# A decoder layer's first feed-forward unit: x and its first weights loaded in quarters over two queues, token squares taken by ScalarE from x as loaded, x in six other PSUM banks

## The chip, the cores and the metric

The kernel runs on one core of one Trainium2 chip. The metric is the device time of one execution in microseconds, and the time before is the median of three runs. The engines are TensorE (PE, matrix products; PEld is its loading of the stationary operand), VectorE (DVE), ScalarE (ACT), GpSimd (POOL) and SyncE (SP, which here only issues transfers).

## What is computed

One layer on x of 512 tokens by 1024 features, all in float32: x plus half a SwiGLU feed-forward, plus a mixer (NSA attention and dilated attention, gated), plus half a second SwiGLU feed-forward, and a final RMSNorm. The change touches only the beginning:

```python
def rmsnorm(x, g):
    y = x32 * lax.rsqrt(jnp.mean(x32 * x32, axis=-1, keepdims=True) + NORM_EPS) * g
...
x = x + 0.5 * swiglu(rmsnorm(x, norm_ffn1[l]), ffn1_w_in[l], ffn1_w_out[l])
```

where `swiglu(h, w_in, w_out)` is `(silu(u) * v) @ w_out` with `u, v` the halves of `h @ w_in` (2 x 2816 columns).

## The kernel before

**Numbers.** Every float32 operand of a large product is split in two rounded parts, `hi` and `lo`, and a product is three passes, hi·hi, lo·hi and hi·lo (`three_pass`, lines 1245 to 1252). ScalarE makes `hi` (an activation Copy into a rounded type), VectorE makes `lo` (original minus `hi`). x is kept transposed, features on partitions, in `xT` (8 feature tiles m of 128 x 512 tokens), times the norm's gain in `xg_hi` and `xg_lo`. The reciprocal root of the mean square is a row over the tokens, so it is not in the operand: it multiplies the products when they are read from PSUM (`rstd_row`, `evac` of `dve_ffn`, line 945).

**Units.** The up projection runs in 22 units of 128 gate and 128 value columns, each 2 x 8 blocks of 128x128 weights, 2 x 512 KB, in two slots of `w_raw`, `w_hi` and `w_lo`. A unit is 48 products of 128x512. SyncE issues the loads of unit f when the low part of unit f-2 is done (`lo_ready`, line 525); ScalarE splits when TensorE has left the slot (`act_split`), VectorE after it (`dve_split`). Unit f from 2 on also waits until the gate of unit f-2 has been scaled (line 1332). The down projection, the mixer and the second feed-forward follow in the same way, each paced by semaphores of the work before.

**The opening** is written out by hand.

- Loads: GpSimd issues the four gains and cmp_pos (five small transfers, lines 621 to 623), all counted on `vec_landed`. SyncE issues x in eight transfers, first the features 0 to 511 for four token blocks, then 512 to 1023 (`x_halves`, line 547), then unit 1. ScalarE issues the constants (with the identity) and unit 0's weights in two halves by feature (`act_load_first`, line 663), then loads its table.
- TensorE (lines 1531 to 1541): five warm-up products on zeros, float32 and so two records each; the transpose of gains and cmp_pos to bank 7, which waits for all five small transfers; 32 transposes of x, tile m to PSUM bank m (`pe_first_transposes`, line 1299), 16 for each half of x; then unit 0.
- Unit 0 goes feature tile by feature tile (`two_products`, line 1290): for each k three passes of gate and three of value into banks 0 and 1. It waits for the half of the low weights and for `g_lo`. As banks 0 and 1 hold x's first two tiles, it also waits until these are copied to `xT` (`x_new`, line 1317).
- Unit 1 accumulates in banks 2 and 3, so it waits for four copies, and for the squares of those tiles. Between its gate and value products stand the column sums (`pe_col`, eight tiny products of `sumsq` with ones) and, after half of the value, the row (`pe_row`, eight products with a diagonal of the reciprocal roots).
- ScalarE (lines 815 to 833): high part of weights half 0; then for each m the high part of x from PSUM (`act_first_hi`), the second weights half after m = 3, and the squares of each feature tile (`act_square`) among them, the high part of unit 1 after m = 6.
- VectorE (lines 1153 to 1173): copy of the gains from bank 7, low part of weights half 0; for each m the low part of x, copies 0 and 1 behind the first two, low half 1 after m = 3; low part of unit 1; copies 2 to 7; then `dve_rstd`.
- GpSimd adds the eight squared feature tiles over m into `sumsq` (`pool_squares`, line 577); the column product then sums over the partitions.

## Time and profile before

| | us |
|---|---|
| median of 3 runs | 1212.22 (1211.77 to 1212.42) |
| the profiled execution | 1211.73 |
| its span in the trace | 1209.9 |
| TensorE busy | 1191.8 (99%) |
| VectorE, ScalarE, GpSimd busy | 570.8, 411.2, 183.2 |

Times in the trace are microseconds from the start of the span. Busy time counts an instruction from its start to its end, and products overlap, so the distance of two starts says more of the pace than their duration. "Idle before <-" names the work that ended an engine's idle time. A timeline merges equal instructions that follow each other (x4). The clock column of the profile shows 1.00 throughout the opening, so the level of TensorE's clock there is read from the distance of its instructions.

### The profile page before, as it was taken

The page shows a single profiled execution, that of the slowest core. Times are in us where ns is not written, and L with a number is a line of the kernel's source. Part 1 is how long each engine was busy: PE and PEld are TensorE (multiplying, and loading weights), DVE is VectorE, ACT ScalarE, POOL GpSimd, SP SyncE. Part 2 cuts the span into 40 slices and gives each one's busy share as a digit, 9 for nine tenths or more (in the row PEclk, how much of TensorE's full clock was granted, in tenths as well). Part 3 has the DMA queues.
Part 4 walks back from the last instruction along what each step waited for, and adds up shares of the span by engine and source line. Part 5 has one row for each costly group of instructions (what it writes and reads, how often), then busy time and mean ns, then how long its engine had stood idle before and what let it go on. Part 6 is the DMA issues. An engine that isn't in the chain of part 4 may idle for free.

```text
span 1209.9 us, 15613 instructions
## 1 busy us (share of the span) xinstructions
PE 1191.8 (99%) x6077; PEld 971.1 (80%) x6077; DVE 570.8 (47%) x898; ACT 411.2 (34%) x578; POOL 183.2 (15%) x205
## 2 busy tenths in 40 slices
PE   8999999999999999999999999999999999999997
PEld 6888888888888988777776788888888888888886
DVE  5544444453333656566656644454544444442222
ACT  5332222322223134443545542233323233222222
POOL 5000000000002571356552000011000000000000
PEclk9999999999999999999999999999999999999998
DMA  7332333223336621222121133333323332223321
GB/s 223 105 94 81 103 104 104 73 81 96 95 107 176 161 77 45 60 60 60 43 75 30 37 95 96 96 105 105 88 86 104 104 102 77 87 76 98 100 84 69
DMA packets 211246, 110.80 MB, mean 92 GB/s; under 512 B 32064, under 2 KB 207600, under 8 KB 211200
## 3 DMA queue, kind: packets, MB, share of 16 engines
q1 hardware_dynamic: 204656, 103.92, 29.9%
q0 software_dynamic: 4288, 5.06, 1.5%
q10 hardware_dynamic: 2256, 1.18, 0.3%
q8 instruction: 32, 0.52, 0.2%
q14 instruction: 14, 0.11, 0.0%
HBM read 105.12 MB, written 2.10 MB: 89 GB/s over the span
## 4 chain that ended last, share of the span: by engine, by line
PE 92%; DVE 4%; ACT 2%; issue 1%; DMA 0%; POOL 0%; DVEq 0%; ACTq 0%; POOLq 0%
PE ps L1250 22%; PE ps L1252 21%; PE ps L1251 21%; PE ps L1358 7%; PE ps L1359 7%; PE ps L1357 7%; PE ps L1460 2%; PE ps L1483 1%; PE ps L1428 1%; PE ps L1441 1%; DVE ps L1056 1%; ACT w_hi L657 1%; DVE w_lo L901 1%; ACT probs L759 1%; PE ps L1495 1%
## 5 line engine op out<-in xcount | busy, mean ns | idle before, releaser
L901 DVE TENSOR_TENSOR w_lo<-w_raw,w_hi 128x2048 fp32r<-128x2048 f32 (+4 forms) x116 | 227.6, 1962 | 410.0 <-ACT w_hi L657 409.7
L1250 PE MATMUL ps<-xg_hi,w_hi 128*128 128x512 f32 x992 | 390.8, 394 | 0.9 <-issue 0.8
L1252 PE MATMUL ps<-xg_hi,w_lo 128*128 128x512 f32 x992 | 386.5, 390 | 0.0
L1251 PE MATMUL ps<-xg_lo,w_hi 128*128 128x512 f32 x992 | 386.3, 389 | 0.0
L657 ACT ACTIVATE w_hi<-w_raw 128x2048 fp32r<-128x2048 f32 (+2 forms) x105 | 182.4, 1737 | 333.4 <-PE ps L1252 210.6
L1250 PEld LDWEIGHTS ps<-xg_hi,w_hi 128*128 128x128 f32 x992 | 186.1, 188 | 48.3 <-issue 10.7
L1252 PEld LDWEIGHTS ps<-xg_hi,w_lo 128*128 128x128 f32 x992 | 186.2, 188 | 39.1
L1251 PEld LDWEIGHTS ps<-xg_lo,w_hi 128*128 128x128 f32 x992 | 186.3, 188 | 37.7
L1357 PE MATMUL ps<-p_hi,w_hi 128*128 128x512 f32 x352 | 137.0, 389 | 0.0
L1359 PE MATMUL ps<-p_hi,w_lo 128*128 128x512 f32 x352 | 137.0, 389 | 0.0
L1358 PE MATMUL ps<-p_lo,w_hi 128*128 128x512 f32 x352 | 136.9, 389 | 0.0
L584 POOL COPY sumsq<-square 128x512 f32<-128x512 f32 x4 | 2.7, 680 | 669.0 <-ACT square L696 666.9
L1357 PEld LDWEIGHTS ps<-p_hi,w_hi 128*128 128x128 f32 x352 | 66.1, 188 | 13.8
L1358 PEld LDWEIGHTS ps<-p_lo,w_hi 128*128 128x128 f32 x352 | 66.1, 188 | 13.7
L1359 PEld LDWEIGHTS ps<-p_hi,w_lo 128*128 128x128 f32 x352 | 66.1, 188 | 13.6
L759 ACT ACTIVATE probs<-ps,stat 128x512 f32<-128x512 f32 (+2 forms) x96 | 51.3, 542 | 73.2 <-DVE stat L1056 73.2
L587 POOL TENSOR_TENSOR sumsq<-sumsq,square 128x512 f32<-128x512 f32 x27 | 38.5, 1426 | 205.8 <-ACT square L696 203.8
L710 ACT ACTIVATE tmp_a<-tmp_a 128x512 f32<-128x512 f32 x44 | 27.8, 632 | 122.9 <-DVE tmp_a L947 122.9
L955 DVE TENSOR_TENSOR p_lo<-tmp_b,p_hi 128x512 f32 (+1 forms) x44 | 30.5, 692 | 38.4 <-ACT p_hi L712 38.4
L598 POOL DMA_DIRECT2D tmp_a<-pool x72 | 38.2, 537 | 56.2 <-DVE pool L1038 53.4
L1056 DVE CUSTOM_DVE_ANT_0 ps<-ps,mask 128x128 f32<-128x128 f32 (+2 forms) x80 | 40.9, 552 | 9.0 <-PE ps L1441 5.7
L1250 PE MATMUL ps<-slot,w_hi 128*128 128x512 f32 x112 | 43.7, 390 | 0.2 <-DVE xT L1228 0.2
(190 smaller groups left out, 1197.5 us busy)
## 6 DMA issues: line engine op xcount, KB each, us to landing
w_raw<-in_ffn_w_in SPq DMA_DIRECT2D x86, 512.0 KB, 4.5
w_raw<-in_w_in SPq DMA_DIRECT2D x32, 512.0 KB, 4.7
w_raw<-in_ffn_w_out SPq DMA_DIRECT2D x32, 384.0 KB, 3.3
w_raw<-in_ffn_w_out SPq DMA_DIRECT2D x32, 320.0 KB, 3.7
w_raw<-in_w_in SPq DMA_DIRECT2D x24, 256.0 KB, 3.9
w_raw<-in_w_out SPq DMA_DIRECT2D x8, 512.0 KB, 3.9
x_nat<-in_x SPq DMA_DIRECT2D x8, 256.0 KB, 6.4
w_raw<-in_w_branch_nsa SPq DMA_DIRECT2D x8, 256.0 KB, 3.9
```

What stands on the lines that cost most here:

```text
L587: nc.gpsimd.tensor_tensor(sumsq[:, :], sumsq[:, :], square[:, m % 2, :], ALU.add).then_inc(acc_done, 1)
L598: pl.dma_start(tmp_a[at + i:at + i + 8, :], x[at + j:at + j + 8, :]).then_inc(swap_landed, 16)
L657: nc.scalar.activation(w_hi[:, s, 0:w], w_raw[:, s, 0:w], ACT.Copy).then_inc(hi_ready, 1)
L759: last = nc.scalar.activation(probs[:, e, i * T + at:i * T + at + w], ps[:, b + i, at:at + w], ACT.Exp, bias=stat[:, e, 1, m:m + 1], scale ...
L901: lo = V.tensor_tensor(w_lo[:, s, c], w_raw[:, s, c], w_hi[:, s, c].bitcast(F32), ALU.subtract)
L1056: return V.tensor_tensor_reduce(out=scores, in0=scores, in1=kept, scale=-SCALE, scalar=least, op0=ALU.add, op1=ALU.min, accum_out=top)
L1250: mm(out, ah, bh, start=(first and i == 0), stop=False)
L1251: mm(out, ah, bl, start=False, stop=False)
L1252: last = mm(out, al, bh, start=False, stop=(final and i == len(pairs) - 1))
L1357: mm(bank, ah, p_hi[:, f, :], start=(f == 0), stop=False)
L1358: mm(bank, ah, p_lo[:, f, :], start=False, stop=False)
L1359: last = mm(bank, al, p_hi[:, f, :], start=False, stop=(f == FT - 1))
```

## The change

- The first gain is loaded alone and first, by ScalarE's queue, and transposed alone (8 rows); the other gains and cmp_pos still come by GpSimd, and are transposed within unit 1, where the column sums of the first norm stood.
- x comes in four quarters by feature, each in two transfers of two token blocks; the second of quarters 1 and 3 by ScalarE's queue, the rest by SyncE's. Unit 0's weights come in four quarters, 0 and 1 by ScalarE's queue, 2 and 3 by SyncE's behind x. Splits of unit 0 are by quarter.
- x's tiles 0 to 5 are transposed to banks 2 to 7, tiles 6 and 7 to banks 2 and 3 after tiles 0 and 1 are copied. Transposes of quarters 2 and 3 of x stand inside unit 0, before feature tiles 2 and 4.
- The squares of the first norm are taken by ScalarE from x as loaded (tokens on partitions), one pass for each of four token blocks, with the sum over the features given out by the same instruction (`accum_out`) into `x_sums`. GpSimd's first eight operations and the first column sums go.
- Unit 1's split is in gate half and value half. Copies 6 and 7 come before it and 2 to 5 after it.
- Three warm-up products instead of five.

```diff
+        def load_x(eng, q, pair):
+            cols, tts = slice(q * D // 4, (q + 1) * D // 4), slice(2 * pair, 2 * pair + 2)
+            eng.dma_start(x_nat[:, tts, cols], x[0].rearrange("(t p) d -> p t d", p=P)[:, tts, cols]).then_inc(x_landed[q], 16)
+        def load_first(eng, h):
+            wi = ktiles(ffn1_w_in[0])
+            for i in range(2):
+                eng.dma_start(first_part(w_raw, h)[:, i],
+                              wi[:, 2 * h:2 * h + 2, i * FF:i * FF + P]).then_inc(part_landed[h] if h < 3 else landed[0], 16)
+        def x_bank(m):
+            return ps[:, 2 + m if m < 6 else m - 4, :]
...
+            def first_loads():
+                for q, pairs in enumerate(((0, 1), (0,), (0, 1), (0,))):
+                    for pair in pairs:
+                        load_x(sp, q, pair)
+                for h in range(2, 4):
+                    load_first(sp, h)
...
-            pl.wait_ge(x_landed[1], 16 * TT)
+            pl.wait_ge(x_landed[3], 32)
             pl.dma_start(cos_t[:, :].bitcast(I32), positions.broadcast_to([P, T])).then_inc(pos_landed, 16)
-            pool_squares(pl, 0)
...
+        def act_split_second(act):
+            act.wait_ge(landed[1], 32)
+            nc.scalar.activation(second_gate(w_hi), second_gate(w_raw), ACT.Copy).then_inc(gate_hi, 1)
+            nc.scalar.activation(w_hi[:, 1, KD * P:SLOT], w_raw[:, 1, KD * P:SLOT], ACT.Copy).then_inc(hi_ready, 1)
+        def act_token_squares(act, tt):
+            if tt:
+                act.wait_ge(acc_done, 2 * tt)
+            nc.scalar.activation(square[:, :, :].rearrange("p a c -> p (a c)"), x_nat[:, tt, :], ACT.Square,
+                                 accum_out=x_sums[:, tt:tt + 1]).then_inc(acc_done, 2)
...
+            act.dma_start(vec_rows[0:KD, :], norm_ffn1[0].rearrange("(m p) -> m p", p=P)).then_inc(gain_landed, 16)
             act.dma_start(const[:, :], consts).then_inc(const_landed, 16)
-            act_load_first(act, 0, half_landed)
-            act_load_first(act, 1, landed[0])
+            load_first(act, 0)
+            load_x(act, 1, 1)
+            load_first(act, 1)
+            load_x(act, 3, 1)
...
             for m in range(KD):
                 act_first_hi(act, m)
-                if m == 3:
-                    act_split_first(act, 1)
-                if m >= 3:
-                    act_square(act, m - 3)
-                if m == KD - 2:
-                    act_split(act, 1)
-            for m in range(KD - 3, KD):
-                act_square(act, m)
+                if m % 2 and m < KD - 1:
+                    act_split_first(act, m // 2 + 1)
+                if m == 5:
+                    for q in range(4):
+                        act.wait_ge(x_landed[q], 32)
+                    act_token_squares(act, 0)
+            act_split_second(act)
+            for tt in range(1, TT):
+                act_token_squares(act, tt)
             act_ffn(act, 0, 0, 0)
...
         def dve_row(dve, n):
             dve.wait_ge(row_psum, n + 1)
             V.tensor_copy(rstd_row[:, :], ps[:, 6, :]).then_inc(row_ready, 1)
+            if n == 0:
+                dve.wait_ge(more_gains, 1)
+                V.tensor_copy(vec_cols[:, KD:64], ps[:, 7, KD:64])
...
-                if m < 2:
-                    V.tensor_copy(xT[:, m, :], ps[:, m, :]).then_inc(x_new, 1)
+                if m % 2 and m < KD - 1:
+                    dve_split_first(dve, m // 2 + 1)
                 if m == 3:
-                    dve_split_first(dve, 1)
-            dve_split(dve, 1)
-            for m in range(2, KD):
-                dve.wait_ge(sq_ready, m + 1)
-                V.tensor_copy(xT[:, m, :], ps[:, m, :]).then_inc(x_new, 1)
+                    dve_first_copy(dve, 0)
+                    dve_first_copy(dve, 1)
+            dve_first_copy(dve, 6)
+            dve_first_copy(dve, 7)
+            dve_split_second(dve)
+            for m in range(2, 6):
+                dve_first_copy(dve, m)
...
+        def pe_first_transposes(pe, q):
+            pe.wait_ge(x_landed[q], 32)
+            for m in range(2 * q, 2 * q + 2):
+                if m == 5:
                     pe.wait_ge(gains_ready, 1)
+                if m > 5:
+                    pe.wait_ge(x_new, m - 5)
                 for tt in range(TT):
+                    last = nc.tensor.transpose(x_bank(m)[:, tt * P:tt * P + P], x_nat[:, tt, m * P:m * P + P], ident)
                 last.then_inc(xt_psum, 1)
+        def pe_other_gains(pe):
+            pe.wait_ge(x_new, KD)
+            pe.wait_ge(vec_landed, 16 * 4)
+            nc.tensor.transpose(ps[:, 7, 0:64], vec_rows[:, :], ident[0:64, 0:64]).then_inc(more_gains, 1)
...
+                elif f == 1:
+                    pe.wait_ge(x_new, 4)
+                    pe.wait_ge(gate_lo, 1)
...
+                        if norm == 0 and k in (2, 4):
+                            pe_first_transposes(pe, k // 2 + 1)
+                        if norm == 0 and k % 2 == 0:
+                            if k < KD - 2:
+                                pe.wait_ge(part_lo, k // 2 + 1)
+                            else:
+                                pe.wait_ge(lo_ready, 1)
...
+                    if norm == 0:
+                        pe.wait_ge(lo_ready, 2)
                     three_pass(ps[:, 2 * s + 1, :], v[:KD // 2], final=False)
...
-            for _ in range(5):
+            for _ in range(3):
                 mm(ps[:, 6, :], tmp_b[:, 0:P], tmp_b[:, :], start=True, stop=True)
             pe.wait_ge(const_landed, 16)
-            pe.wait_ge(vec_landed, 16 * 5)
-            nc.tensor.transpose(ps[:, 7, 0:64], vec_rows[:, :], ident[0:64, 0:64]).then_inc(gains_psum, 1)
+            pe.wait_ge(gain_landed, 16)
+            nc.tensor.transpose(ps[:, 7, 0:KD], vec_rows[0:KD, :], ident[0:KD, 0:KD]).then_inc(gains_psum, 1)
```

The rest of the diff renames semaphores, lowers counts that the first norm's squares and column sums had raised (`sq_ready`, `col_psum`), and takes four columns of padding for `x_sums`, so that the tiles behind it stay where they were.

## Rows read from the trace of the kernel before

**Rows 1.** The page's chain that ended last, by engine.
```profile
PE 92%; DVE 4%; ACT 2%; issue 1%; DMA 0%; POOL 0%; DVEq 0%; ACTq 0%; POOLq 0%
```
**Rows 2.** Busy time from unit 2 on: stretch, length, us (count) of each engine, clock, DMA, GB/s.
```profile
core 0: us, PE busy (x) PEld busy (x) DVE busy (x) ACT busy (x) POOL busy (x), PEclk, DMA share, GB/s
38.73:1209.90 1171.17, 1156.39 (x5923) 944.87 (x5921) 548.30 (x863) 393.44 (x554) 167.71 (x187) 1.00 0.31 89
```
**Rows 3.** The chain of waits in the first 16 us: start, us, what.
```profile
3.50 5.77 DMA vec_rows<-in_cmp_pos
...
9.41 0.26 PE ps L1538
...
13.85 0.50 PE ps L1250
```
**Rows 4.** Timeline of TensorE's products, 24 to 39 us: start, us, engine, line, operation, tiles.
```profile
24.64 0.39 PE L1252 MATMUL ps<-xg_hi,w_lo 128*128 128x512 f32 x1
...
25.83 0.47 PE L1250 MATMUL ps<-xg_hi,w_hi 128*128 128x512 f32 x1 [0.81 <-issue]
...
31.39 0.95 PE L1263 MATMUL ps<-const,sumsq 128*128 128x2 f32 x8
32.20 0.49 PE L1250 MATMUL ps<-xg_hi,w_hi 128*128 128x512 f32 x1
...
38.73 0.39 PE L1250 MATMUL ps<-xg_hi,w_hi 128*128 128x512 f32 x1
```
**Rows 5.** Transfers issued from 0.7 to 1.3 us: how many, KB each, us to landing.
```profile
const<-shape_constants ACTq DMA_DIRECT2D x1, 130.0 KB, 3.8
vec_rows<-in_norm_ffn POOLq DMA_DIRECT2D x1, 4.0 KB, 4.7
```
**Rows 6.** Timeline of VectorE.
```profile
11.20 0.74 DVE L1163 SCALAR_TENSOR_TENSOR xg_lo<-ps,vec_cols,xg_hi 128x512 fp32r<-128x512 f32 x1
...
15.03 1.33 DVE L907 TENSOR_TENSOR w_lo<-w_raw,w_hi 128x1024 fp32r<-128x1024 f32 x1
...
21.23 3.30 DVE L901 TENSOR_TENSOR w_lo<-w_raw,w_hi 128x2048 fp32r<-128x2048 f32 x1
...
32.38 0.16 DVE L922 TENSOR_SCALAR norm_s<-ps 128x4 f32<-128x4 f32 x1 [4.25 <-PE ps L1263]
...
33.82 0.88 DVE L934 TENSOR_SCALAR tmp_a<-const,rstd_col 128x128 f32<-128x128 f32 x4
```
**Rows 7.** Timeline of ScalarE (ACTq: its issues of transfers).
```profile
1.20 2.30 ACTq L666 DMA_DIRECT2D w_raw<-in_ffn_w_in  x4
3.53 1.28 ACT L820 ACT_TABLE_LOAD   x1 [3.53 <-issue]
...
8.90 1.06 ACT L671 ACTIVATE w_hi<-w_raw 128x1024 fp32r<-128x1024 f32 x1 [3.87 <-DMA w_raw<-in_ffn_w_in]
10.35 2.42 ACT L676 ACTIVATE xg_hi<-ps,vec_cols 128x512 fp32r<-128x512 f32 x4 [0.39 <-PE ps L1305]
```
**Rows 8.** Busy time in three stretches of the opening; the last number is GB/s.
```profile
0.00:5.00 5.00, 3.50 (x4) 1.51 (x5) 0.54 (x2) 1.46 (x2) 2.98 (x9) 1.00 0.63 183
5.00:7.00 2.00, 2.00 (x4) 0.89 (x3) 0.00 (x0) 0.03 (x1) 0.00 (x0) 1.00 0.99 298
7.00:9.00 2.00, 1.74 (x4) 0.43 (x3) 0.00 (x0) 0.10 (x1) 0.00 (x0) 1.00 1.08 384
```
**Rows 9.** DMA queues from 0 to 8.9 us (q1 SyncE's, q10 ScalarE's): packets, MB, share.
```profile
q1 hardware_dynamic: 786, 1.44, 49.7%
q10 hardware_dynamic: 1402, 0.76, 29.0%
```
**Rows 10.** Timeline of TensorE's weight loads and products, 0 to 14 us.
```profile
1.50 0.50 PEld L1535 LDWEIGHTS ps<-tmp_b 128*128 128x128 f32 x2 [1.50 <-DVE tmp_b L1155]
...
5.93 0.34 PEld L1535 LDWEIGHTS ps<-tmp_b 128*128 128x128 f32 x1 [0.52 <-issue]
6.78 0.27 PEld L1535 LDWEIGHTS ps<-tmp_b 128*128 128x128 f32 x1 [0.52 <-issue]
7.29 0.19 PEld L1535 LDWEIGHTS ps<-tmp_b 128*128 128x128 f32 x1 [0.24 <-issue]
...
9.59 1.97 PE L1305 MATMUL ps<-const,x_nat 128*128 128x128 f32 x16
```

More of the change, by code:

```diff
@@ L250, in build @@
         lo_ready = sem("weight_lo_ready")
[L251 to L253 removed]
+        part_landed = [sem(f"first_unit_part_landed_{h}") for h in range(3)]
+        part_hi = sem("first_unit_part_hi_ready")
+        part_lo = sem("first_unit_part_lo_ready")
+        gate_hi = sem("second_unit_gate_hi_ready")
+        gate_lo = sem("second_unit_gate_lo_ready")
+        gain_landed = sem("first_gain_landed")
+        more_gains = sem("other_gains_in_psum")
         cleared = sem("warm_up_operands_cleared")
@@ L258, in build @@
         vec_landed = sem("gains_and_cmp_pos_landed")
-        x_landed = [sem(f"x_features_landed_{h}") for h in range(2)]
+        x_landed = [sem(f"x_features_landed_{h}") for h in range(4)]
         gains_psum = sem("gains_in_psum")
```

101 lines of the change are left out of this document (42 added, 59 removed).

## The prediction

> **What bounds the kernel now.** I read the page first: TensorE holds 92% of the chain that ended last [rows 1]. The reader should see that only a microsecond in which TensorE has no product to run can be won. Then the windows: from 38.73 us, where unit 2 begins, to the end, TensorE is busy for 1156.4 of 1171.2 us [rows 2], and none of that is edited except waits whose counts change. So the change must pay in the first 38.73 us, and what it pays there reaches the end unchanged: after unit 2 every load waits for a split, every split for a unit, none for a fixed time. Then the chain in the opening: it stands until 9.27 on five small GpSimd transfers of gains and cmp_pos (the last is issued at 3.50 and lands 5.77 later), the gains' transpose is at 9.41, and behind it come the DVE's low part of the first weights, low part of x, copy, low part, copy, and the first real product at 13.85 [rows 3]. The copies are there because x's first two banks are the accumulators of unit 0. So three things hold TensorE back: a gain that arrives at 9.3, x in halves, and the copies.
>
> The TensorE timeline gives the rest. After unit 0 the next product would have started at 24.87 and starts at 25.83: 0.96 us, for unit 1 waits for four x copies, which the DVE begins only behind an undivided low part of unit 1's weights that ran 3.30 us from 21.23 beside GpSimd's additions [rows 4, 6]. The eight column-sum products take from 31.39 to 32.20, plus about 0.1 of slower restart (0.49 against 0.39 for the product behind them) [rows 4].
>
> **The change, part by part.** *Loads.* The gain comes first on ACT's queue (4 KB; the constants of 130 KB landed 3.8 us after issue at 0.75, the small gain transfer of GpSimd 4.7 after its issue [rows 5]), so both are there by about 5.5. ACT now issues eight transfers instead of five: three more at about 0.5 each (its four weight issues took 2.30 in all) end at about 4.9 instead of 3.5, so table load (1.28) and warm-up (0.20) end at about 6.4, and the high part of quarter 0 of the weights, half of the 1.06 that half the unit takes, at 7.0 [rows 7]. That is ahead of the gain (below), so I cost the issues at nothing; without that cover they would cost 1.4. SP issues x in six transfers and then four quarter transfers before unit 1's two: at the same 0.5 each, quarter 1 of x is issued by 2.2 and the last weight quarter by 5.8, well ahead of the bytes in front of them.
>
> When does x arrive? All queues together moved 183 KB/us up to 5 us, 298 up to 7 and 384 up to 9 [rows 8]: 0.91 MB by 5, 1.51 by 7, 1.90 by 8. Up to 8.9 SP's queue had moved 1.44 MB in 786 packets and ACT's 0.76 MB in 1402 [rows 9]: where both have work, packets alternate, and SP's 2 KB rows outran ACT's 512 B rows. Quarters of x come in 1 KB rows, so SP now gets about two bytes for ACT's one beside weights, and equal shares beside x. Quarter 0 of x (524 KB on SP) is moved when 0.86 MB are, at 4.8; weights quarter 0 with 1.06 MB, at 5.5; x quarter 1 with 1.31 to 1.58 MB, at 6.4 to 7.2. A landing comes about 0.3 later: x quarter 1 at 7.1, by the other bound (all shares scaled like the first weights half, which landed at about 8.9 with 2.2 MB moved where 1.7 MB stood ahead of it [rows 7, 9]) at 8.0. Quarters 2 and 3 of x follow at about 9 and 10.5, of the weights at 9.3, 11.1, 11.8, unit 1 at 15.6, since the total is the same.
>
> *Start.* Three warm-up products instead of five. Each is two records, each record's weight load starts one record ahead, and these loads are 0.85 us apart (5.93 for the seventh, 6.78 for the eighth, 7.29 for the ninth: there it is 0.51) [rows 10]: six records end at 1.50 + 6 x 0.855 = 6.63, and there the gain's transpose now starts, not at 9.41. From that transpose to the first high part of x it was 0.94 (9.41 to 10.35 [rows 3, 7]); the pass takes 0.65 until the DVE can start, the low part 0.74 [rows 6]: 6.65 + 0.94 + 0.65 + 0.74 + 0.1 = 9.1. No copies (1.2 us) stand between, since banks 0 and 1 are free, and the DVE's low part of the weights is 0.6 for a quarter, done before. TensorE meanwhile runs the transposes of x quarters 0 and 1: 16 took 1.97 [rows 10], from 6.8 to 8.8 if quarter 1 is there by 7.8. So the first product is at 9.1. The bounds: 8.5, if the clock rises earlier and ACT's 7.0 becomes the limit; 10.6, if all 16 transposes run at half speed (3.7 us from 6.9).
>
> *Unit 0 to unit 2.* Before, 24.88 us (13.85 to 38.73). The transposes of quarters 2 and 3 move from ahead of unit 0 into it: 2 x 0.98, and 0.1 each for the slower restart: +2.15. The wait before unit 1 goes: -0.96. The column sums go (-0.90); one transpose of 64 rows stands in their place, between 0.12 (one of sixteen) and 0.4: +0.3. Sum 25.4, so unit 2 starts at 9.1 + 25.4 = 34.5 instead of 38.73: **4.2 us less**.
>
> *The covers.* The pace of unit 0 is 1.36 us a feature tile (six products of 0.227; twenty-four took 5.56 with their restart, from 25.83 to 31.39 [rows 4]). The DVE needs a low part of x (0.66) and half a weight quarter (0.31), the ACT 0.58 and 0.27 [rows 6, 7]: both keep ahead. At tile 2 (11.9) and tile 4 (15.6) TensorE transposes quarters landed at 9 and 10.5; for tile 6 it waits for copies 0 and 1, done about 13.8. Copies 6 and 7 end about 19.4, the gate half of unit 1's low part about 20.7, and unit 1 starts at 22.3. The value half ends about 22, the last copy about 24.4, needed at 27.8. The token squares are four ACT passes of 128x1024 with a sum, between 1.06 (the copy of that size [rows 7]) and twice that, I take 1.2, near the row of the same size, three of them after 19.5: done about 23.2, so they hide, and the eight GpSimd additions that stretched the DVE's low part to 3.30 are gone. The Newton steps and diagonal take 2.3 after the last copy (32.38 to the last of the diagonal at 34.70 [rows 6]): 26.7, needed at 30.9. The row's products end at 31.7; its copy, that of the other gains and the scaling of the gate (under 0.74 each, the low part's time of 512 columns [rows 6], the second of 56 columns far under) end by 33.5, before unit 2 at 34.5. SP loads unit 2 after the last quarter's low part, 15.8 instead of 16.4.
>
> **The clock, against the change.** The weight loads show the level rise between 6.78 and 7.29, while the seventh record ran, from 1.2 to 2.4 GHz, after unbroken products since 1.50 [rows 10]. The four records that are removed are those in and behind the rise; in their place stand one small transpose and sixteen of x, with a possible pause for x. I take it that these keep the rise where it is, since there is no pause if x quarter 0 is there by 6.7. The Trainium skill (TensorE: Matmul & The Clock Gate, "What's actually happening") says that the half-rate state is the default and that only sustained activity releases it. By that page a pause in the transposes could leave the first unit at the lower level, and the sum would be that of rival (a) or (c) instead of 1208.0; the row at least agrees that the run began at the lower level. What either would cost is worked out from rows below.
>
> **Rivals.** (a) *The clock rises late.* Sixteen transposes at half speed end at 10.6, +1.5; twelve first products at half speed cost 12 x 0.227 = 2.7 more: gain 0 to 2.7, 1209.5 to 1212. For it: the warm-up loses 40%. Against: work of the same kind follows at once. 8%. (b) *x or operands come late.* The DMA engines were already moving 384 KB/us with both queues at work [rows 8], so x quarter 1 may land at 8.5 to 9.5, or tiles 2, 4 and 6 may each wait 0.3 to 0.5 for their hand-offs over ACT and DVE: 1 to 1.7 lost, gain 2.5 to 3.2, 1209.0 to 1209.7. 14%. (c) *Slower.* The clock stays low through all of unit 0, because TensorE stops for x after quarter 0's transposes: 32 transposes (+3.9, of which 0.4 is hidden) and 48 products (+10.9) make some 14 against 4.2, so 1222; it decides from about 9 us of work spent at the lower level on (4.2 gained, 0.5 lost in each, within a slack of 0.2). Against: the rise came after 5.5 us of products, and twelve products follow 9.1. 4%. (d) *Hidden anyway:* that unit 2 must wait for its low part or the row, which would return the 4.2. By the times above its low part is ready about 29, 5 us early, the gate scaled 1 us early. Gain 0 to 1: 3%. The forecast itself, gain 3.4 to 5: 71%.
>
> **The numbers.** The profiled execution took 1211.73 (span 1209.9), 0.5 under the median of 1212.22 and just below the spread of the runs, 1211.77 to 1212.42. Against the median 4.2 less is 1208.0. The range has the early start at its low end (4.8, with 0.4 for restarts and the gains' transpose at their lower bounds and 0.3 for the scatter of the runs: 1206.7), and (b) and the near part of (a) at its high end, 1209.8. A measurement of this kernel can tell about 0.2%, 2.4 us, from no change. Faster: forecast, (b), and a quarter of (a), 0.87; same: rest of (a), (d), 0.09; slower 0.04.
>
> **What would show it.** In the profile after: gain transpose at 6.6 to 6.7; first product of unit 0 at 9.1; two blocks of eight transposes within unit 0, 0.95 to 1.1 us each; no idle ahead of unit 1; one short transpose where the column sums were; unit 2 at 34.5; TensorE from there to the end as before, 1171.2 us. Wrong would be: a weight load distance of 0.2 instead of 0.11 in the transposes, idle ahead of tiles 2, 4 or 6 with a DMA or the ACT as releaser, or the 4 us won by unit 2 and missing at the end.

## The result, and the profile after

The changed kernel takes 1217.63 us (median of 22 runs, 1212.87 to 1219.66), the kernel before 1213.18 (22 runs beside them, 1211.77 to 1215.68): ratio 1.0032 with a 95% interval of 1.0023 to 1.0040. Slower by 4.5 us, where 1208.0 was forecast. The profiled execution took 1217.66, its span is 1215.8, so it stands for the median. The profiled execution of the kernel before, with its span of 1209.9, took 1211.73, less than each of the 22, so 5.9 us lie between the two profiles where 4.5 lie between the medians. All ratios below compare undisturbed runs; one execution of 3138 us of the kernel with five warm-ups is left out.

The opening first. Timeline of TensorE in the changed kernel (start us, us, engine, line, operation, tiles, count, idle time ahead and what ended it):

```profile
1.50 5.49 PE L1590 MATMUL ps<-tmp_b 128*128 128x512 f32 x6 [1.50 <-DVE tmp_b L1198]
6.92 0.27 PE L1593 MATMUL ps<-const,vec_rows 8*128 8x8 f32 x1
7.13 1.10 PE L1350 MATMUL ps<-const,x_nat 128*128 128x128 f32 x8
10.53 1.96 PE L1350 MATMUL ps<-const,x_nat 128*128 128x128 f32 x8 [2.30 <-DMA x_nat<-in_x]
12.14 0.78 PE L1295 MATMUL ps<-xg_hi,w_hi 128*128 128x512 f32 x1
12.71 0.63 PE L1296 MATMUL ps<-xg_lo,w_hi 128*128 128x512 f32 x1
...
14.23 0.39 PE L1297 MATMUL ps<-xg_hi,w_lo 128*128 128x512 f32 x1
...
31.29 0.27 PE L1356 MATMUL ps<-const,vec_rows 64*128 64x64 f32 x1
31.49 0.50 PE L1295 MATMUL ps<-xg_hi,w_hi 128*128 128x512 f32 x1
...
34.35 1.05 PE L1312 MATMUL ps<-tmp_a,const 128*128 128x128 f32 x8
...
37.99 0.39 PE L1295 MATMUL ps<-xg_hi,w_hi 128*128 128x512 f32 x1
```

The gain's transpose is at 6.92 (forecast 6.6, in [rows 3] it was at 9.41). Then TensorE transposes x quarter 0 and stands still for 2.30 us, until the half of quarter 1 that ScalarE's queue carries has landed. The chain of waits of the same kernel shows that transfer as one piece:

```profile
2.84 7.64 DMA x_nat<-in_x
```

It is issued at 2.84 and lands at 10.48, not at 7.1. And in the pause the clock is lost: the granted clock is 1.2 GHz from 10.57 to 13.98, right behind 2.30 us without a product. The transposes of quarter 1 take nearly twice as long as those of quarter 0, and the first products start 0.43 to 0.57 apart instead of 0.23. So the first product comes at 12.14 instead of 9.1, and unit 2 begins at 37.99: 0.74 earlier than before [rows 4], not 4.2. That is most of the forecast gain gone.

The rest of the result is behind unit 2. From there to the end it is 1215.8 - 37.99 = 1177.8 us against 1171.2 [rows 2]: 6.6 us lost in a stretch in which nothing was edited. Windows of the changed kernel, then of the kernel before (stretch; length; busy us and count of PE, PEld, DVE, ACT, POOL; granted clock; DMA share; GB/s):

```profile
9.00:14.00 5.00, 3.47 (x13) 3.09 (x14) 2.93 (x5) 3.10 (x6) 0.10 (x1) 0.66 1.15 313
...
540.00:550.00 10.00, 8.61 (x34) 5.67 (x32) 4.45 (x16) 4.11 (x13) 5.75 (x7) 0.83 0.61 111
640.00:655.00 15.00, 12.85 (x67) 9.16 (x66) 9.35 (x20) 6.48 (x15) 4.37 (x3) 0.77 0.24 55
```

```profile
9.00:14.00 5.00, 4.26 (x34) 3.75 (x35) 4.17 (x7) 4.35 (x7) 0.59 (x1) 1.00 1.12 363
...
540.00:550.00 10.00, 8.69 (x51) 5.48 (x49) 5.82 (x19) 4.95 (x15) 6.01 (x7) 1.00 0.52 113
640.00:655.00 15.00, 13.54 (x106) 9.78 (x105) 12.24 (x31) 6.17 (x20) 1.98 (x1) 1.00 0.21 54
```

Two things are to be seen. In the last two stretches the clock is 0.83 and 0.77 where it was 1.00: it falls to 1.2 GHz from 543.05 to 546.46 and from 645.45 to 652.27, and this execution of the kernel before has no such fall. Others of its executions do. In the 146 that ran beside the experiments the mean granted clock goes from 0.993 to 0.998, and the time with it, from 1215.4 us on average at 0.993 to 1212.2 at 0.997; the 22 of the changed kernel have 0.989 to 0.995. So falls became more frequent, but they are not new. And in the first stretch the DMA engines are as busy as before (1.15 and 1.12) while they move 313 GB/s instead of 363. The pause ahead of the second fall, in the timeline of the changed kernel and then of the kernel before:

```profile
645.47 1.54 PE L1515 MATMUL ps<-const,probs 128*128 128x128 f32 x6 [2.15 <-DVE probs L1164]
```

```profile
642.90 0.88 PE L1460 MATMUL ps<-const,probs 128*128 128x128 f32 x6 [1.46 <-DVE probs L1121]
```

Setting the same instructions of both traces beside each other gives the ledger behind unit 2: the fall at 543 costs 1.6, the pauses at 585 and 606 another 0.5 each (0.34 before and 0.83 after at the first; none and 0.35 at the second, with its slower restart), the pause at 645 0.7, the fall behind it 3.2. Sum 6.5 of 6.6. Two items of this ledger can't be put down to what is found below. The pause at 585 is 0.64 to 0.91 us in all eleven kernels that have the diff and 0.34 to 0.35 in all nine that don't, whatever their DMAs did. And a fall near 543 to 546 also came in two kernels with packets as fast as before (b_pad184, behind a pause of 1.22, and a_pad48), and did not come in four with slow ones, one of them behind a pause of 1.61 (b_pad64). The fall at 645 is different: it came in all nine kernels with slow packets, behind pauses of 1.81 to 2.25 us, and in none of the eleven others, with 0.76 to 1.67.

The stretch around these falls is the attention, where GpSimd fetches row swaps by DMA and waits for them. The instructions that use the pool tile, of the changed kernel and of the kernel before (who waited for it: us, times):

```profile
  POOL tmp_a L628: 19.5, 9
```

```profile
  POOL tmp_a L601: 13.8, 7
```

The DMA queue of SyncE in the page of the changed kernel and of the kernel before (packets, MB, share of 16 engines):

```profile
q1 hardware_dynamic: 206224, 103.92, 32.1%
```

```profile
q1 hardware_dynamic: 204656, 103.92, 29.9%
```

The same 103.92 MB in 0.8% more packets took 1215.8 x 32.1 against 1209.9 x 29.9, 8% more engine time. By the packet records a 512-byte packet on SyncE's queue between 9 and 16 us took 32.0 ns on average instead of 27.0, between 520 and 640 us 31.6 instead of 29.3, over the whole kernel 29.8 instead of 28.0; a 256-byte packet 23.4 instead of 18.9, and the 2 KB packets of the row swaps 124 instead of 110. (The median of the 512-byte packets of the whole kernel is 27 in both: a part of them got slower, most of all where both queues are at work.) So transfers had become slower until the end, although the diff only touched the first 25 us.

### The profile page after: what moved, and what is told of

Same layout as the page of the kernel before. It is cut to its first block, busy times and chain, and to the rows that moved or that the text cites. A ratio compares the mean times of both kernels' runs of the same rounds, so it can differ in the third digit from the quotient of the medians.

```text
span 1215.8 us, 15588 instructions
## 1 busy us (share of the span) xinstructions
PE 1195.3 (98%) x6066; PEld 974.1 (80%) x6066; DVE 572.2 (47%) x902; ACT 411.8 (34%) x581; POOL 170.3 (14%) x196
## 3 DMA queue, kind: packets, MB, share of 16 engines
q1 hardware_dynamic: 206224, 103.92, 32.1%
## 4 chain that ended last, share of the span: by engine, by line
PE 92%; DVE 4%; ACT 2%; issue 1%; DMA 1%; ACTq 0%; DVEq 0%
PE ps L1295 22%; PE ps L1297 21%; PE ps L1296 21%; PE ps L1412 7%; PE ps L1414 7%; PE ps L1413 7%; PE ps L1515 2%; PE ps L1538 1%; PE ps L1496 1%; DVE w_lo L924 1%; PE ps L1483 1%; DVE ps L1099 1%; ACT w_hi L683 1%; ACT probs L778 1%; PE ps L1550 1%
## 5 line engine op out<-in xcount | busy, mean ns | idle before, releaser
L924 DVE TENSOR_TENSOR w_lo<-w_raw,w_hi 128x2048 fp32r<-128x2048 f32 (+5 forms) x115 | 224.4, 1951 | 408.6 <-ACT w_hi L683 408.4
L683 ACT ACTIVATE w_hi<-w_raw 128x2048 fp32r<-128x2048 f32 (+3 forms) x104 | 180.5, 1736 | 335.7 <-PE ps L1297 212.8
L1414 PEld LDWEIGHTS ps<-p_hi,w_lo 128*128 128x128 f32 x352 | 66.1, 188 | 13.8
L614 POOL TENSOR_TENSOR sumsq<-sumsq,square 128x512 f32<-128x512 f32 x20 | 27.1, 1357 | 203.9 <-ACT square L715 203.9
L1099 DVE CUSTOM_DVE_ANT_0 ps<-ps,mask 128x128 f32<-128x128 f32 (+2 forms) x80 | 40.9, 552 | 10.9 <-PE ps L1496 5.8
```

The lines of the kernel that those rows point to most:

```text
L683: nc.scalar.activation(w_hi[:, s, 0:w], w_raw[:, s, 0:w], ACT.Copy).then_inc(hi_ready, 1)
L924: lo = V.tensor_tensor(w_lo[:, s, c], w_raw[:, s, c], w_hi[:, s, c].bitcast(F32), ALU.subtract)
L1099: return V.tensor_tensor_reduce(out=scores, in0=scores, in1=kept, scale=-SCALE, scalar=least, op0=ALU.add, op1=ALU.min, accum_out=top)
L1414: last = mm(bank, al, p_hi[:, f, :], start=False, stop=(f == FT - 1))
```

## The experiments

### Is it only the timing? Four kernels

Theory A: the attention is sensitive to when it starts, so that moving unit 2 by 0.7 us is what loses the clock. Theory B: something that stays until the end is slower.

**Before, with eight products added just ahead of unit 2.** `norm == 0` is the first norm.

```
+            if norm == 0:
+                for _ in range(8):
+                    mm(ps[:, 5, :], xg_hi[:, 0, 0:P], xg_hi[:, 1, :], start=True, stop=True)
```

> The kernel before with eight such products (1.8 us) at the same place. Theory A: the attention comes 1.8 us later, so other falls than before: the median is off the plain sum by over 1 us, or the runs scatter as those of the changed kernel do (over 3 us). Theory B: 1213.2 + 1.8 = 1215.0 us with the scatter of before.

Measured: 1213.25 against 1213.75, ratio 1.0000 (0.9992 to 1.0009). Unit 2 starts 2.2 us later and the end is 1.5 later by the profile, 0 by the medians. No fall of the clock; the pause at the end of the attention shrank from 1.46 to 0.76:

```profile
644.31 0.88 PE L1463 MATMUL ps<-const,probs 128*128 128x128 f32 x6 [0.76 <-DVE probs L1121]
```

Part of 1.8 us of real work added in the opening came back by itself later. The median is 1.8 us off the plain sum of theory B, which the expectation had put down to theory A; the scatter (1211.9 to 1215.4) is that of the kernel before. So this run alone favours theory A; the next one decides.

**After, with three such products (`range(3)`), which bring unit 2 about back to its old time.**

> The changed kernel with three more products of 128x512 (0.68 us, results unused) between unit 1 and unit 2 of the first feed-forward, so that everything behind runs at the times it had before the change. Theory A (the loss sits in stretches of the attention where TensorE's clock falls to 1.2 GHz, and whether it falls hangs on when the stretch comes): the falls go or become as rare as before, 1212.2 to 1214.5 us although work was added. Theory B (a lasting cost of the change behind unit 2, whatever the time): 1217.6 + 0.7 = 1218.3 us.

Measured: 1217.38, ratio 1.0031 (1.0019 to 1.0044), clock low at 11.1 to 14.5, 543.6 to 550.4 and 649.4 to 656.2. Unit 2 starts at 39.2 in its profile, 0.4 later than before, and nothing recovers, though the time is also 0.9 under the 1218.3 of theory B. As the explanation of the loss theory A falls.

**After, with five warm-up products again.**

```
-            for _ in range(3):
+            for _ in range(5):
```

> The changed kernel with the two warm-up products put back. Both theories: TensorE then works until about 8 us and waits for x only some 1.5 us instead of 2.3, so the clock stays at 2.4 GHz over 10.6 to 14.0 us; eight transposes and the first four products take half the time, unit 2 begins at about 36.2 instead of 38.0. Theory B: 1217.6 - 1.8 = 1215.8 us. Theory A: somewhere from 1210 (no fall later) to 1217 (as many falls as in the changed kernel).

Measured: 1216.21, ratio 1.0015 (1.0006 to 1.0023), about 1.4 less than the change. That is near the 1215.8 of theory B, but not by the expected way: in the profile TensorE stood from 9.31 to 11.86 for the same half of x, the clock was low from 12.5 to 15.9 and three times more later, and unit 2 began at 39.4 where 36.2 was expected. The profiled execution is the slowest of the eleven (1219.51), so it doesn't stand for the median. In it, more warm-up didn't carry the clock over a pause of 2.5 us.

**After, with all of x on SyncE's queue.**

```
-                for q, pairs in enumerate(((0, 1), (0,), (0, 1), (0,))):
+                for q, pairs in enumerate(((0, 1), (0, 1), (0, 1), (0, 1))):
...
-            load_x(act, 1, 1)
             load_first(act, 1)
-            load_x(act, 3, 1)
```

> The changed kernel with all of x on SyncE's queue (ScalarE's queue: gain, constants, weight quarters 0 and 1). My reading: x quarter 1 came at 10.5 us because its second half stood behind 512-byte rows of weights on the queue that got the smaller share; alone on SyncE's queue it lands at 7.5 to 8.5, the first product is at 9.3 to 9.8 and unit 2 at about 35. Rival (the DMA engines as a whole were the limit): quarter 1 no earlier than 10, unit 2 at 37.5 or later. Total: by theory B 1214.6 us, by theory A 1208.5 (no fall later) to 1216.

Measured: 1213.89, ratio 1.0003 (0.9992 to 1.0014). Quarter 1 of x is there at 8.3, so the rival (the DMA engines as a whole) falls. The sixteen transposes run without a pause, the clock stays up in the opening, unit 2 begins 2.5 us earlier than in the kernel before. The expected 9.3 to 9.8 for the first product was not reached, though: it came at 11.19, behind 1.72 us without work, for the low part of x on VectorE, and behind that stands the weights' quarter 0, which landed at 8.93 on ScalarE's queue. Then most of the gain is lost again: swaps waited 19.6 us, the pause at the end of the attention is 2.03 and the clock falls behind it, 642.5 to 645.9. So the late half of x explains 1.8 us of the opening (unit 2 at 36.2 instead of 38.0), and the loss behind unit 2 is another one.

### A wrong guess: the small GpSimd transfers

The change takes one small transfer off GpSimd, whose queue also issues the swaps. Theory C: their count decides how the swaps' packets fall on the engines. Each kernel adds small loads into a tile not yet in use, and the wait for the positions counts them:

```
+            for i in range(1):
+                pl.dma_start(sin_t[8 * i:8 * i + 8, 0:P], norm_mix[0].rearrange("(m p) -> m p", p=P)).then_inc(pos_landed, 16)
```

> The changed kernel with one more small transfer by GpSimd (a gain of 8 rows to rows of sin_t that nothing uses yet), issued behind the positions, so that GpSimd has again issued four transfers of 8 rows before the attention, as before the change, not three. Theory C (where the next small transfer of GpSimd goes among the DMA engines hangs on how many it has issued; the change took one away, and since then the swaps of rows for the rotary embedding land later): GpSimd's idle time on landed swaps falls from about 20 us to the 13.8 us of before, TensorE's waits at about 584 and 642 us fall to 0.35 and 1.5 us, fewer falls of the clock, 1211.5 to 1213.5 us. Theory D (the swaps are late because everything comes at another time, or by chance): as the changed kernel, about 19 to 20 us and 1216 to 1218 us.

> The changed kernel with all of x on SyncE's queue (unit 2 at 36.25 us in the profile of that kernel, 2.5 us ahead of before) and the fourth small transfer of GpSimd. Theory C: 2.5 us under before, with as few falls of the clock: 1209.5 to 1212. Theory D: as the kernel with x on SyncE's queue alone, 1213.9 us.

> The kernel before with one such transfer added behind the positions (five of 8 rows). Theory C: the swaps land late as in the changed kernel (19 to 20 us of idle time on them), TensorE's waits at 584 and 642 us are 0.7 and 2.1 us, the clock falls more often: 1215 to 1218 us, though the opening is untouched. Theory D: as before, 13.8 us and 1212 to 1214.3 us.

> The kernel before with two such transfers added (six of 8 rows). Theory C, with an order that alternates between two places: as before, 13.8 us of idle time on the swaps, 1212 to 1214.3 us. If any added transfer hurts: 1215 to 1218 us or more. Theory D: as before.

Measured: the change with one more 1218.4 (ratio 1.0038), the version with x on one queue and one more 1213.91 (1.0013), before with one and two more 1213.93 and 1213.76 (1.0008 and 1.0004, both intervals with 1 in them). Nothing follows the count. The swaps waited 19.2 and 20.5 us in kernels with the diff, 14.1 and 14.7 in those without. Theory C falls.

### The 32 bytes

Left was what the diff does to the addresses. It adds `x_sums`, four fp32 columns (16 bytes), and takes four columns from a padding of 56. The printed addresses of the tiles show what came of it: every tile takes a multiple of 32 bytes. 52 columns are 208 bytes and still take 224, as 56 did; `x_sums` takes 32. So all tiles behind the padding stand 32 bytes higher: the raw weights at 67616 instead of 67584, x at 138784 instead of 138752, the pool at 151072 instead of 151040. Before, each of these was a multiple of 512 (138752 is 271 x 512); now none is. Theory E: the shift slows the DMAs and costs about 0.3% by itself.

**Before with 64 columns of padding (32 bytes more), nothing else.**

```
-            sb("pad_before_operands", [P, 56])
+            sb("pad_before_operands", [P, 64])
```

> The kernel before with 64 instead of 56 columns of padding: all from xg_hi on 32 bytes later, as in the changed kernel, nothing else. Theory E: 29 to 32 ns a packet, 19 to 20 us of idle time on swaps, waits at 584 and 642 us 0.7 and 2.1 us: 1215 to 1219 us. Theory D: 1212 to 1214.3 as before.

Measured: 1217.82 against 1213.7, ratio 1.0031 (1.0021 to 1.0041). That is as much as the whole loss of the change (1.0032), from one number in the kernel before. Its windows, its pause at the end of the attention, its swaps and SyncE's queue:

```profile
9.00:14.00 5.00, 3.89 (x33) 3.55 (x33) 3.61 (x6) 3.43 (x5) 0.59 (x1) 1.00 1.13 327
...
640.00:655.00 15.00, 12.77 (x69) 9.10 (x67) 8.97 (x19) 6.43 (x16) 4.75 (x4) 0.77 0.23 56
```

```profile
645.87 1.54 PE L1460 MATMUL ps<-const,probs 128*128 128x128 f32 x6 [2.23 <-DVE probs L1121]
```

```profile
  POOL tmp_a L601: 20.8, 8
```

```profile
q1 hardware_dynamic: 204656, 103.92, 31.9%
```

The same packets as before, in number and bytes, and 31.9% of the engines where it was 29.9%; 512-byte packets between 9 and 16 us take 32.3 ns. The wait ahead of unit 1 grows from 0.81 [rows 4] to 1.46, and the clock falls from 645.9 to 652.7. The wait at 585, expected at 0.7, stayed at 0.35. The engines themselves are no slower at the shifted addresses: by the two pages the mean of a split on VectorE is 1968 ns where it was 1962, on ScalarE 1737 in both, of a hi·hi product 394 in both. So the loss comes over the DMAs.

**Which alignment is wanted.** Padding of 72, 88, 120 and 184 columns: 64, 128, 256 and 512 bytes more than before. In the last the padding further back was cut, so that x and the mixer's tiles stay where they were.

> The kernel before with 72 columns of padding: all from xg_hi on 64 bytes later. If alignment to 64 bytes is what counts: as before, 1212 to 1214.3 us and 27 ns. If any shift from the tuned place costs: 1215 to 1219.

> The kernel before with the padding 88 columns wide instead of 56, which moves the tiles behind it by 128 bytes. Theory 'a shift of 32 or 64 bytes is what costs, 128 is enough': 512-byte packets on SyncE's queue 27.0 ns as in the kernel before, 1212 to 1214 us. Rival 'it takes 256 bytes or a multiple': packets 32 ns, about 1217.8 us, ratio 1.003. Between the two (29 to 30 ns, 1215 to 1216) would mean that the price falls off with the shift.

> The kernel before with 120 columns of padding: all from xg_hi on 256 bytes later. 32 and 64 bytes both cost 0.31%. If a multiple of 512 bytes, the length of a weight row in a transfer, is what counts: 1215 to 1219 us, 512-byte packets at about 32 ns in 9 to 16 us. If 128 or 256 is enough: 27 ns and 1212 to 1214.3 us.

> The kernel before with 184 columns of padding ahead of xg_hi (512 bytes more) and 64 instead of 192 columns ahead of x_nat, so that operands and weights sit 512 bytes later and x_nat, p_hi and the mixer's tiles where they were. If alignment to 512 bytes (or less) counts: as before, 27 ns and 1212 to 1214.3 us. If only the very place counts: 1215 to 1219.

| shift, bytes | 512-byte packet, 9 to 16 us | swaps waited, us | this / before, us | ratio, 95% interval |
|---|---|---|---|---|
| 0 | 27.0 ns | 13.8 | | |
| 32 | 32.3 | 20.8 | 1217.82 / 1213.7 | 1.0031, 1.0021 to 1.0041 |
| 64 | 32.4 | 18.8 | 1217.84 / 1213.7 | 1.0031, 1.0022 to 1.0040 |
| 128 | 33.2 | 18.3 | 1215.39 / 1213.68 | 1.0022, 1.0010 to 1.0034 |
| 256 | 27.0 | 15.7 | 1212.15 / 1213.86 | 0.9990, 0.9981 to 0.9999 |
| 512 (operands) | 27.0 | 13.8 | 1214.0 / 1213.86 | 1.0007, 0.9999 to 1.0016 |

It is a step and not a slope: the packets are slow at 32, 64 and 128 bytes and as before at 256 and 512. Of the two expectations on 128 bytes the rival's packet time held, and its time came out between the two. The Trainium skill has the rule (DMA: Bandwidth & Descriptors, "How a descriptor splits into AXI transactions"): a descriptor is cut into transactions of 256 bytes, each starting at a multiple of 256, so one that starts elsewhere needs one more. By that a row of 512 bytes takes three in the place of two. The page speaks of reads and gives no time; here the shifted side is the written one, and the runs agree with it in the place of the step, with 27.0 against 32 to 33 ns. By their size they agree only in part: the rows of 256 bytes lose most over the whole kernel (18.9 to 23.1 ns on average with 32 bytes of shift), those of 512 bytes go from 28.0 to 29.7 with a median of 27 in both, and packets of 96 bytes stay at 12.0.

**The change with the padding at 48 columns**, the alignment restored.

```
-        sb("pad_before_operands", [P, 52])
+        sb("pad_before_operands", [P, 48])
```

> The changed kernel with 48 instead of 52 columns of padding. The allocator gives every tile a multiple of 32 bytes, so x_sums (16 bytes) took 32 and the padding gave up none: everything from xg_hi on sits 32 bytes later than before (34848 for 34816). 48 columns put it back. Theory E (DMA writes to tiles shifted by 32 bytes are slower: 512-byte packets took 32.0 ns instead of 27.0 at 9 to 16 us, and the row swaps land up to 1.3 us later, which lengthens TensorE's waits in the attention and lets the clock fall): packets at 27 ns, GpSimd's idle time on swaps 13 to 15 us instead of 19.5, waits at 584 and 642 us 0.35 and 1.5 us, x quarter 1 earlier than 10.5 us; in all at or under the kernel before, 1208 to 1213. Theory D (the slower packets come of the order of the loads or the transfers' number): as the changed kernel, 1216 to 1218.

Measured: 1213.65 against 1213.7, ratio 0.9998 (0.9990 to 1.0007). 27.0 ns, and 4 us of the loss are gone. No gain is left. In the profiled execution, 1.9 us above the median, x's half on ScalarE's queue landed still later. Timeline of TensorE:

```profile
6.79 1.09 PE L1350 MATMUL ps<-const,x_nat 128*128 128x128 f32 x8
11.83 1.97 PE L1350 MATMUL ps<-const,x_nat 128*128 128x128 f32 x8 [3.95 <-DMA x_nat<-in_x]
13.45 0.78 PE L1295 MATMUL ps<-xg_hi,w_hi 128*128 128x512 f32 x1
```

The clock is low from 9.68 to 16.51, and unit 2 starts 1.2 us later than in the kernel before. In the six kernels with x on both queues this half landed between 10.5 and 11.8. Falls of the clock at 450.0 and 545.6 in this kernel, with packets of 27.0 ns, show that the shift is not their only cause.

**The same with `range(5)`: five warm-ups.**

> The changed kernel with the alignment restored and five warm-up products. The share of the clock in the opening: with three, TensorE stood 3.95 us for x quarter 1 and the clock was at 1.2 GHz from 9.7 to 16.5 us, 1.7 us of which in eight transposes and seven products counted. If five keep it up: 1213.65 - 1.7 = 1212 us. If the wait for x (until 10.5 to 11.8) is still long enough for a fall: 1213.5.

Measured: 1211.6, ratio 0.9985 (0.9976 to 0.9994). Here x landed at 10.5, the longer warm-up left a pause of 0.84 only, and the clock stayed up: first product at 11.36, unit 2 2.3 us before the old time. x landed 1.3 us earlier here than in the profile with three, so the profiles alone don't separate the two. The medians do, twice: with x on both queues five warm-ups took 1211.6 against 1213.65 for three, and with the shift 1216.21 against 1217.63. With x late, the two removed warm-ups were cover.

### What the change could give: three kernels

**Padding of 48 columns, and all of x on SyncE's queue** (the two edits shown above).

> The changed kernel with 48 columns of padding and all of x on SyncE's queue. Theory E: packets at 27 ns, weight quarter 0 (the last to land there, at 8.9 us) some 0.5 us earlier, unit 2 at about 35.8 us, and the attention as before: 1209.5 to 1211.5 us, 2 to 3.5 under before. Theory D: 1213.9 as with the queue alone.

Measured: 1209.14 against 1213.7, ratio 0.9964 (0.9951 to 0.9976; 5 runs). Timeline of TensorE:

```profile
6.76 1.09 PE L1348 MATMUL ps<-const,x_nat 128*128 128x128 f32 x8
8.44 1.09 PE L1348 MATMUL ps<-const,x_nat 128*128 128x128 f32 x8 [0.59 <-DMA x_nat<-in_x]
10.92 0.47 PE L1293 MATMUL ps<-xg_hi,w_hi 128*128 128x512 f32 x1 [1.39 <-DVE xg_lo L1204]
...
13.75 1.04 PE L1348 MATMUL ps<-const,x_nat 128*128 128x128 f32 x8
14.54 0.47 PE L1293 MATMUL ps<-xg_hi,w_hi 128*128 128x512 f32 x1
```

Quarter 1 of x is there at 8.4; now the first product waits for the weights' quarter 0, which landed at 8.66 on ScalarE's queue. ScalarE has its high part of x queued behind that wait.

**The value half of the weights' quarter 0 moved too**, to SyncE's queue behind x quarter 0.

```
-        def load_first(eng, h):
+        def load_first(eng, h, halves=(0, 1)):
...
+                    if q == 0:
+                        load_first(sp, 0, (1,))
...
-            load_first(act, 0)
+            load_first(act, 0, (0,))
```

> As ax_pad48 (alignment restored, all of x on SyncE's queue; 1209.14), and the value half of weight quarter 0 moved from ScalarE's queue to SyncE's behind x quarter 0. There the first product (10.92 us) stood behind weight quarter 0, landed at 8.66. Expected: it lands at 7.5 to 8, x quarter 1 about 0.4 later (8.8), first product at 10.0 to 10.3, total 0.5 to 0.9 less: 1208.4. If x quarter 1 becomes the last: no gain, 1209.1.

Measured: 1209.69 against 1213.86, ratio 0.9973 (0.9964 to 0.9982).

```profile
6.35 1.09 PE L1350 MATMUL ps<-const,x_nat 128*128 128x128 f32 x8
9.17 1.09 PE L1350 MATMUL ps<-const,x_nat 128*128 128x128 f32 x8 [1.73 <-DMA x_nat<-in_x]
10.02 0.48 PE L1295 MATMUL ps<-xg_hi,w_hi 128*128 128x512 f32 x1
```

First product at 10.0, unit 2 at 35.05, 3.7 us before the old time, and the clock full until the last microseconds. By the profile it is the best (span 1206.6, against 1207.2 for the version above); by the medians the two can't be told apart.

**The same with five warm-ups.**

> The version with the alignment restored, all of x on SyncE's queue and the value half of the first weights behind x's first quarter on that queue, with five warm-ups in the place of three. Theory 'with x there at 9.1 us the three warm-ups are enough': TensorE's clock is full at the first product in both, the first product stays near 10.0 us, unit 2 near 35.1, and the time at 1209 to 1210 us, not to be told from three warm-ups. Rival 'the idle time of 1.7 us before the first product still costs something': first product and unit 2 come earlier or the time falls by over 1 us, to about 1208.

Measured: 1210.65 against 1213.68, ratio 0.9978 (0.9969 to 0.9987). The clock is full at the first product either way; that product comes at 10.72 instead of 10.02, since the longer warm-up now stands in front of the transposes. With x on time three warm-ups are enough.

## Why the prediction was wrong

**The step that failed first was none of its steps.** The text ahead of the prediction took the padding as keeping the tiles behind it where they were, and the prediction costed nothing there. It moved them by 32 bytes, which by itself costs 0.31% (b_pad64), 4.1 us: as much as the whole forecast gain. Between the forecast difference of -4.2 and the measured +4.5 lie 8.7 us. Taking the shift out of the changed kernel gives 4.5 of them back against the kernel before (a_pad48, ratio 0.9998), and putting all of x on one queue another 4.5 (ax_pad48; five executions only). The addresses are in the kernel's allocations and could have been added up, with the rounding of each tile.

**"What it pays there reaches the end unchanged ... none for a fixed time"** was the second failed step, and [rows 2] could not carry it: 1156.4 busy of 1171.2 us says that 15 us are idle, not what those wait for. The idle intervals of TensorE over 0.1 us behind unit 2 sum to 6.7 us, 5.9 of them between 400 and 660 us, around the attention. One of them hangs on GpSimd's swaps, grows with slower packets and can take the clock with it (3.2 of the 6.6 us). The b_late8 run shows the other sign: about 2 us later at unit 2 cost nothing in the median. Where no fall of the clock and no slow packet stood behind unit 2, the step held nearly: 2.8 us won at unit 2 gave a span 2.7 shorter (ax_pad48), 3.7 gave 3.3 (axs_pad48).

**The arrival of x was mis-sized.** Forecast 7.1, with 8.0 as the other bound; measured 10.5 to 11.8 with the shift, 10.5 and 11.8 without. So the shift is not its reason. Two terms were wrong. The total was too high: the trace has 1.02 MB by 6 us and 1.60 by 8, where the forecast took 1.90 by 8. The constants' issue now comes behind the gain's, at 1.42 instead of 0.75, so ScalarE's queue starts late. The 1.58 MB that the forecast wanted moved were moved at about 8.0, which makes 8.3 with its 0.3 for the landing. The other 2.2 us are the order: the forecast asked only when enough bytes had passed, not whose. Up to 8.0 us ScalarE's queue had moved 0.42 MB in 722 packets where SyncE's had moved 1.16 MB in 1199, and both transfers of x's quarter 2 landed (8.24 and 9.97) before the second half of quarter 1. "Packets alternate" held only where both queues had work all the time: 188 and 186, 219 and 219, 302 and 307 packets in the three microseconds from 8 on, of which SyncE's were mostly rows of 1 KB at first. A shared total doesn't order two queues: what is needed first has to be first on its own queue, with few bytes in front. Moving the half to SyncE's queue brings it to 8.4 or 9.1. The Trainium skill says of the shared engines (DMA: Bandwidth & Descriptors, "Issuing engines are not separate DMA queues") that a second issuing engine saves only issue time. The runs go further than the page: with the same padding, x on one queue took 1209.14 (five executions) and on two 1213.65 (twelve), so the second queue cost time.

**The clock.** Rivals (a) and (b) came true together: x came later than (b) allowed, and TensorE stood for it behind quarter 0's transposes, which is the condition of rival (c). The price of the low level was as stated in (a), 0.2 us for each product: 0.9 in unit 0 and nearly as much in the second eight transposes. The forecast "these keep the rise where it is" held as long as work followed: the clock was full from 7.16 on, just behind the warm-ups, and the two aligned kernels with three warm-ups and x on one queue didn't lose it before the last microseconds, one of them over a pause of 1.73. It was the pause, which the two missing warm-ups made longer. The size of rival (c), the clock low through all of unit 0, did not come: 3.4 us low, 6.8 at the worst (a_pad48).

**What held.** The gain's transpose came at 6.92, in the three kernels with three warm-ups and the alignment restored at 6.2 to 6.6 (forecast 6.6). From the first product to unit 2 25.4 was forecast (its terms add up to 25.5), measured 25.0 in both fast versions (10.92 to 35.95, 10.02 to 35.05), and in the changed kernel 25.85, of which 0.9 is the low clock. Its terms: two blocks of transposes inside unit 0 at 0.8 each with the restart (13.75 to 14.54 above) where 1.08 was taken; no wait ahead of unit 1; one transpose of 0.2 (31.29 to 31.49) in the place of 0.9 of column sums. The covers of squares, copies and Newton steps held. So of the distance from 4.2 to what ax_pad48 gives, 2.8 at unit 2, the arrival of x and of the weights' quarter 0 is all: the first product at 10.9 instead of 9.1, less 0.4 from the sum behind it. Both could be mended in part, and the whole then reaches 4.6 and 4.2 us in the medians (ax_pad48, axs_pad48), the size that was forecast. That match is partly chance: by the profiles it is 2.7 and 3.3, and unit 2 never came the forecast 4.2 earlier.

**Where the range failed.** It ended at 1209.8, with the rest of (a) and (d) above it up to 1212. It had no case in which a part that is not in the opening becomes slower; only rival (c) had a time above the old one, for another reason.

**How slow packets reach TensorE.** The pause ahead of 645 us goes with the packets over all kernels: with packets of 27.0 ns the swaps waited 12.7 to 16.6 us in all and this pause was 0.76 to 1.67, with 32 to 33 ns 18.3 to 20.8 and 1.81 to 2.25. The traces show the link. In the kernel before, GpSimd waits 2.60 us for a swap and then multiplies; VectorE meanwhile has a sum of one element per partition to make, on the way to the `probs` that TensorE waits for:

```profile
631.82 1.27 POOL L601 TENSOR_TENSOR tmp_a<-tmp_a,sin_t 128x512 f32<-128x512 f32 x1 [2.60 <-DMA tmp_a<-pool]
632.66 0.45 DVE L1117 TENSOR_TENSOR stat<-stat 128x1 f32<-128x1 f32 x1
```

In the changed kernel the swap lands 0.66 us later against VectorE's work, and the same sum takes 1.10:

```profile
634.36 1.27 POOL L628 TENSOR_TENSOR tmp_a<-tmp_a,sin_t 128x512 f32<-128x512 f32 x1 [3.26 <-DMA tmp_a<-pool]
634.54 1.10 DVE L1160 TENSOR_TENSOR stat<-stat 128x1 f32<-128x1 f32 x1
```

Fourteen of the sixteen such sums in each of these two traces take 0.15 to 0.16 us; the two that run beside an operation of GpSimd take longer. In all 20 traces this one ends within 0.1 us of the end of a GpSimd operation, and in 19 the pause is 0.96 to 1.06 us plus what the sum took. In the twentieth (b_late8) both GpSimd operations were over before the scaling of `probs` that follows, which took 0.62 us instead of 1.58, and the pause was the shortest. So a later swap holds VectorE longer, and VectorE holds TensorE. No run changed the swaps alone.

Still open: why the pause at 585 grew with the diff, and why the clock falls near 543 in some kernels and not in others with the same pause. Nor is it settled why that half of x landed 1.3 us apart in two aligned kernels with the same queues: the order was the same, and in the later one (a_pad48) ScalarE's queue was behind already at 6 us, with 0.18 MB against 0.22.

## What to carry to other kernels

When a change adds or resizes a tile, add up the addresses behind it as the allocator rounds them, and keep the targets of DMAs with rows of 256 or 512 bytes at multiples of 256: that was worth 0.3% of a kernel that is bound by TensorE at 92% of its chain. A transfer that is wanted early belongs on the queue that starts first, ahead of everything wanted later; splitting it over two queues makes it wait for the slower one. And price a pause of TensorE with the clock that may go with it: 2.3 us without a product cost about 1.7 us more in slow work behind it.

## What was not expected of the hardware

A shift of 32, 64 or 128 bytes of the written side slowed 512-byte packets in the opening from 27.0 to 32 or 33 ns, at the same number of packets; 256 and 512 didn't. A slower DMA reached a kernel whose DMA engines are about 30% used: a swap that lands 0.66 us later makes a one-element sum on VectorE take 1.10 us instead of 0.45 beside GpSimd's work, and the pause of TensorE behind it, 1.81 to 2.25 us, came with a fall from 2.4 to 1.2 GHz for 3.4 to 6.8 us in all nine kernels that had it. And 1.8 us of products added to the opening of the kernel before changed its median by nothing (ratio 1.0000, 0.9992 to 1.0009).
